# Broadcast load of the norm weights in the opening, two waits at seams placed otherwise, and 354 columns in two conv units: a hybrid conv and retention layer in fp32

## What is computed

```python
hn = rmsnorm(h, norm_mix_w)
proj = hn @ w_in                                   # 1024 x 3584
xt, b_gate, c_gate, q, k, v, g = jnp.split(proj, IN_SPLITS, axis=-1)
ucat = jnp.concatenate([conv_hist, c_gate * xt], axis=1)
conv_y = conv_w[0] * ucat[:, :T] + conv_w[1] * ucat[:, 1:T + 1] + conv_w[2] * ucat[:, 2:]
conv_out = b_gate * conv_y
...                                                # rotary q, k; chunked retention with decay; group norm
ret_out = jax.nn.silu(g) * o
h = h + jnp.concatenate([conv_out, ret_out], axis=-1) @ w_out
f = jnp.square(jax.nn.relu(rmsnorm(h, norm_ffn_w) @ w_up)) @ w_down
return h + f, new_hist, new_state
```

## Time and profile before

| | us |
|---|---|
| median of 3 runs (1237.04 to 1238.17) | 1237.44 |
| profiled execution, its own time | 1237.57 |
| its span from first to last instruction | 1235.3 |
| TensorE busy (99% of the span) | 1220.2 |
| TensorE weight loads | 1121.9 |
| DVE, ACT, POOL busy | 746.5, 494.7, 296.3 |
| TensorE's last matmul ends at about | 1226.6 |
| mean granted TensorE clock | 0.997 |

### The profile page before, as it was taken

The page is one execution under the profiler, slowest core; times in us unless marked ns, Lnnn a source line. Parts: engine busy times, 40 slices in busy tenths (PEclk is TensorE's granted clock), DMA queues, the critical chain, the costliest instruction groups (busy, mean ns, idle before and its releaser), DMA issues.

```text
span 1235.3 us, 20174 instructions
## 1 busy us (share of the span) xinstructions
PE 1220.2 (99%) x6674; PEld 1121.9 (91%) x6674; DVE 746.5 (60%) x1337; ACT 494.7 (40%) x1031; POOL 296.3 (24%) x230
## 2 busy tenths in 40 slices
PE   8999999999999999999999999999999999999997
PEld 5889999999999888989989989988998998998995
DVE  5435564465555453386676677568568667667747
ACT  5413213213232342355335435534543533543456
POOL 2000000000000000143543452352453354335212
PEclk9999999999999999999999999999999999999998
DMA  6011111111111630122021021111202202102103
GB/s 243 28 34 39 39 47 38 47 45 30 47 38 57 188 112 1 52 60 69 8 68 59 8 68 59 37 39 59 68 9 59 68 8 68 59 8 68 51 18 145
DMA packets 85117, 69.57 MB, mean 56 GB/s; under 512 B 9425, under 2 KB 68945, under 8 KB 85090
## 3 DMA queue, kind: packets, MB, share of 16 engines
q1 hardware_dynamic: 85090, 69.21, 18.2%
HBM read 64.21 MB, written 4.99 MB: 56 GB/s over the span
## 4 chain that ended last, share of the span: by engine, by line
PE 96%; DVE 2%; ACT 1%; issue 1%; DMA 1%; POOL 0%; POOLq 0%; SPq 0%; DVEq 0%; ACTq 0%
PE ps L1445 29%; PE ps L1447 29%; PE ps L1446 29%; PE ps L1451 1%; PE ps L1452 1%; PE ps L1462 1%; PE ps L1556 1%; PE ps L1633 1%; PE ps L1574 1%; PE ps L1563 1%; PE ps L1573 1%; PE ps L1469 0%; DMA dr<-in_w_down 0%; DVE hw L1353 0%; PE ps L1580 0%
## 5 line engine op out<-in xcount | busy, mean ns | idle before, releaser
L1445 PE MATMUL ps<-mid_hi,ws_hi 128*128 128x368 f32 (+1 forms) x768 | 251.3, 327 | 1.1 <-DVE ws_lo L1225 1.1
L1447 PE MATMUL ps<-mid_hi,ws_lo 128*128 128x368 f32 (+1 forms) x768 | 251.4, 327 | 0.0
L1446 PE MATMUL ps<-mid_lo,ws_hi 128*128 128x368 f32 (+1 forms) x768 | 250.8, 327 | 0.0
L1269 DVE TENSOR_TENSOR h<-ps,h 128x512 f32<-128x512 f32 x300 | 193.8, 678 | 8.5 <-PE ps L1447 8.5
L1445 PE MATMUL ps<-hn_hi,ws_hi 128*128 128x368 f32 (+1 forms) x576 | 194.4, 337 | 1.0 <-ACT v_all L616 1.0
L1447 PE MATMUL ps<-hn_hi,ws_lo 128*128 128x368 f32 (+1 forms) x576 | 189.5, 329 | 0.0
L1446 PE MATMUL ps<-hn_lo,ws_hi 128*128 128x368 f32 (+1 forms) x576 | 189.3, 329 | 0.0
L1393 POOL TENSOR_TENSOR h<-tmp,h 128x512 f32<-128x512 f32 x120 | 159.1, 1357 | 125.6 <-ACT tmp L817 125.6
L1445 PE MATMUL ps<-do_hi,fo_hi 128*128 128x512 f32 x452 | 176.2, 390 | 0.0
L1447 PE MATMUL ps<-do_hi,fo_lo 128*128 128x512 f32 x452 | 176.0, 389 | 0.0
L1446 PE MATMUL ps<-do_lo,fo_hi 128*128 128x512 f32 x452 | 176.0, 389 | 0.0
(11 more groups left out here) (198 smaller groups left out, 1826.1 us busy)
## 6 DMA issues: line engine op xcount, KB each, us to landing
raw<-in_w_up SPq DMA_DIRECT2D x64, 256.0 KB, 4.9
dr<-in_w_down SPq DMA_DIRECT2D x64, 256.0 KB, 3.5
raw<-in_w_in SPq DMA_DIRECT2D x48, 256.0 KB, 2.9
xr<-in_x_prompt SPq DMA_DIRECT2D x8, 512.0 KB, 4.0
raw<-in_w_out SPq DMA_DIRECT2D x16, 256.0 KB, 3.2
out<-hw SPq DMA_DIRECT2D x16, 256.0 KB, 2.1
wv_raw<-in_w_in SPq DMA_DIRECT2D x8, 256.0 KB, 5.2
h<-in_x_prompt SPq DMA_DIRECT2D x2, 1024.0 KB, 11.5
```

Source lines behind the costliest of these rows:

```text
L1269: dve.tensor_tensor(h_part(p, q), bank_of(p, q)[:, :], h_part(p, q), ALU.add).then_inc(dve_add, 1)
L1445: pe.matmul(out, a_hi, b_hi, start=start, stop=False, skip_group_check=again)
L1446: pe.matmul(out, a_hi, b_lo, start=False, stop=False, skip_group_check=again)
L1447: return pe.matmul(out, a_lo, b_hi, start=False, stop=stop, skip_group_check=again)
```

## The change

- The weights of the first norm are loaded by one broadcast DMA of 512 KB straight into `normw`, issued behind x tile 0. `norm_row`, `ones`, two matmuls and two DVE copies go; TensorE issues `keep_warm(5)` in place of 1 + 2 matmuls + 2.
- The order of the v weights' splits: ACT makes tile 0's hi parts after slice 1, then slices 2, 3, 4, then `root(1)`. DVE takes slices 0, 1, 2, 4, 6, POOL 3, 5, 7.
- TensorE waits for all but the last v tile ahead of the loop; the last one's wait stands before unit q, once in each turn of the loop.
- The memset of `h[:, 8]` moves ahead of the waits in `residual(4)`.
- ACT's group 0 is written out in front of its loop in an order of its own: relus of block 0 and the split of block 1's second half first, then all seven D splits.
- The last two meta rows are now the first two of the 16 in the row order (`META_AT`; positions and decays follow it, and x tile 8 comes in three DMAs). Units xt and c compute only these: their third column group is 354 wide in place of 368, and ACT and DVE copy 2 columns where they copied 16.

```diff
 CGQ = [(0, 368), (368, 368), (736, 352)]
+CGC = [(0, 368), (368, 368), (736, 354)]
+META_AT = [META - 2, META - 1, *range(META - 2)]
 CGY = [(0, 368), (368, 368), (736, 352)]
...
 UNITS = [("k", 3 * DC + DC, CGX), ("q", 3 * DC, CGQ), ("g", 3 * DC + 3 * DC, CGQ),
-         ("xt", 0, CGX), ("c", 2 * DC, CGX), ("b", DC, CGQ)]
+         ("xt", 0, CGC), ("c", 2 * DC, CGC), ("b", DC, CGQ)]
 V_OFF = 3 * DC + 2 * DC
+WV_DVE = [0, 1, 2, 4, 6]
+WV_POOL = [3, 5, 7]
 NU = len(UNITS)
...
     inv = (np.float32(10000.0) ** (-np.arange(half, dtype=np.float32) / np.float32(half))).astype(np.float32)
-    pos = np.concatenate([np.arange(SEQ), np.arange(SAMPLE) + PAST, np.arange(META) - META]).astype(np.float32)
+    pos = np.concatenate([np.arange(SEQ), np.arange(SAMPLE) + PAST, np.array(META_AT) - META]).astype(np.float32)
     ang = (pos[None, :] * inv[:, None]).astype(np.float32).astype(np.float64)
...
         head[h, :, C_KDEC] = np.exp((P - 1 - j) * lg) * scale
-        head[h, SAMPLE:SAMPLE + META, C_KMETA] = np.exp((META - 1 - j[:META]) * lg) * scale
+        head[h, SAMPLE:SAMPLE + META, C_KMETA] = np.exp((META - 1 - np.array(META_AT)) * lg) * scale
         head[h, :SAMPLE, C_KSAMP] = np.exp((SAMPLE - 1 - j[:SAMPLE]) * lg) * scale
...
             out = []
-            for src, a, b in ((xp_d, 0, SEQ), (xs_d, SEQ, TY), (meta_d, TY, TX)):
+            for src, a, b in ((xp_d, 0, SEQ), (xs_d, SEQ, TY), (meta_d[META - 2:META, :], TY, TY + 2), (meta_d[0:META - 2, :], TY + 2, TX)):
                 s, e = max(lo, a), min(hi, b)
...
-            sp.dma_start(norm_row[:, :], norm_mix_w[0:1, :]).then_inc(row_in, 16)
             load_x(0)
+            sp.dma_start(normw[:, :], norm_mix_w[0:1, :].broadcast_to([P, D])).then_inc(row_in, 16)
             sp.dma_start(ident[:, :], c_ident).then_inc(const_in, 16)
...
             wv_hi_part(1)
+            hi_parts(0)
             wv_hi_part(2)
-            hi_parts(0)
             wv_hi_part(3)
+            wv_hi_part(4)
             root(1)
-            for k in range(4, KT):
+            for k in range(5, KT):
                 wv_hi_part(k)
...
                     act.activation(u[:, META + SEQ + 2:TX + 2], bank[:, m:m + SAMPLE], ACT.Copy)
-                    act.activation(u[:, 0:META], bank[:, m + SAMPLE:n], ACT.Copy).then_inc(proj_act, 1)
+                    act.activation(u[:, META - 2:META], bank[:, m + SAMPLE:n], ACT.Copy).then_inc(proj_act, 1)
...
-            def group(g):
+            def group(g, first):
                 act.wait_ge(prod_done, NPROD * g + 1)
                 up_split(g, "up", 0)
-                d_hi(g, "B11")
-                d_hi(g, "T1")
-                d_hi(g, "B21")
-                d_hi(g, "T3")
-                act.wait_ge(f_ready, NF_PARTS * g + 1)
-                relu(g, 0, 0)
-                d_hi(g, "B22")
-                square(g, 0, 0)
-                relu(g, 0, 1)
-                d_hi(g, "T2")
-                relu(g, 0, 2)
-                up_split(g, "up", 1)
-                d_hi(g, "T4")
+                if first:
+                    relu(g, 0, 0)
+                    square(g, 0, 0)
+                    relu(g, 0, 1)
+                    relu(g, 0, 2)
+                    up_split(g, "up", 1)
+                    for name in D_HI:
+                        d_hi(g, name)
+                else:
+                    d_hi(g, "B11")
+                    d_hi(g, "T1")
+                    d_hi(g, "B21")
+                    d_hi(g, "T3")
+                    act.wait_ge(f_ready, NF_PARTS * g + 1)
+                    relu(g, 0, 0)
+                    d_hi(g, "B22")
+                    square(g, 0, 0)
+                    relu(g, 0, 1)
+                    d_hi(g, "T2")
+                    relu(g, 0, 2)
+                    up_split(g, "up", 1)
+                    d_hi(g, "T4")
                 square(g, 0, 1)
...
-            with act.Fori(0, G_LAST) as g:
-                group(g)
+            group(0, True)
+            with act.Fori(1, G_LAST) as g:
+                group(g, False)
...
             dve.memset(on[:, :, :], 0.0).then_inc(warm_ready, 1)
-            dve.memset(ones[:, :], 1.0).then_inc(warm_ready, 1)
...
-            dve.wait_ge(row_done, 1)
-            dve.tensor_copy(normw[:, 0:512], ps[1][:, :])
-            link(dve.tensor_copy(normw[:, 512:1024], ps[4][:, :]))
+            dve.wait_ge(row_in, 16)
             normed(0)
             wv_lo_part(0)
+            wv_lo_part(1)
             lo_parts(0)
             wv_lo_part(2)
+            wv_lo_part(4)
             normed(1)
-            wv_lo_part(4)
             wv_lo_part(6)
...
                         dve.tensor_tensor(u[:, META + SEQ + 2:TX + 2], bank[:, m:m + SAMPLE], u[:, META + SEQ + 2:TX + 2], ALU.mult)
-                        ins = dve.tensor_tensor(u[:, 0:META], bank[:, m + SAMPLE:n], u[:, 0:META], ALU.mult)
+                        ins = dve.tensor_tensor(u[:, META - 2:META], bank[:, m + SAMPLE:n], u[:, META - 2:META], ALU.mult)
                     ins.then_inc(proj_dve, 1)
...
                 n = rows(t)
+                if p == 4:
+                    dve.memset(h[SAMPLE:P, TILES - 1, :], 0.0)
                 dve.wait_ge(out_done, p + 1)
...
                     dve.wait_ge(h_rest_in, 32)
-                    dve.memset(h[SAMPLE:P, TILES - 1, :], 0.0)
                 pair = OUT_PAIRS[p]
...
             pool.memset(smC[:, :], 0.0).then_inc(pad_ready, 1)
-            for k in range(1, KT, 2):
+            for k in WV_POOL:
                 pool.wait_ge(wv_hi_ready, k + 1)
...
                     if t == 0:
-                        pe.wait_ge(wv_lo_pool if k % 2 else wv_lo_dve, k // 2 + 1)
+                        pe.wait_ge(wv_lo_pool, WV_POOL.index(k) + 1) if k in WV_POOL else pe.wait_ge(wv_lo_dve, WV_DVE.index(k) + 1)
                     elif k == 0 and t >= 2:
...
             pe.wait_ge(warm_ready, 1)
-            keep_warm(1)
-            pe.wait_ge(warm_ready, 2)
-            pe.wait_ge(row_in, 16)
-            pe.matmul(ps[1][:, :], ones[:, :], norm_row[:, 0:512], start=True, stop=True)
-            pe.matmul(ps[4][:, :], ones[:, :], norm_row[:, 512:1024], start=True, stop=True).then_inc(row_done, 1)
-            keep_warm(2)
+            keep_warm(5)
             pe.wait_ge(const_in, 16)
...
                 v_part(t, range(6, KT))
-            pe.wait_ge(v_taken, XTILES)
+            pe.wait_ge(v_taken, XTILES - 1)
...
                 elif name == "q":
+                    if j == 0:
+                        pe.wait_ge(v_taken, XTILES)
                     pe.wait_ge(proj_dve, i * 12 + 9 + j + 1)
```

More of the change, by code:

```diff
@@ L203, in build @@
         junk = sb("junk", [P, D], r3)
-        r_y = region(TY * 4)
-        y = sb("y", [P, TY], r_y)
-        norm_row = sb("norm_row", [1, D], r_y)
+        y = sb("y", [P, TY], region(TY * 4))
         cos_t = sb("cos_t", [P, TX], region(TX * 4))
@@ L216, in build @@
         onC = sb("onC", [P, HD], region(512))
-        r_rot = region(BLK * 4)
-        rot = sb("rot", [P, BLK], r_rot)
-        ones = sb("ones", [1, P], r_rot)
+        rot = sb("rot", [P, BLK], region(BLK * 4))
         hc = sb("hc", [P, NCONST], region(NCONST * 4))
@@ L250, in build @@
         row_in = sem("row_in")
-        row_done = sem("row_done")
         wv_in = [sem(f"wv_in{n}") for n in range(KT)]
```

## The result

| | before | after |
|---|---|---|
| median, us | 1237.57 (1237.04 to 1238.17, 6 runs) | 1228.97 (1228.24 to 1229.79, 6 runs) |
| ratio | | 0.9931, 95% interval 0.9918 to 0.9943 |
| profiled execution, its span | 1237.57, 1235.3 | 1229.5, 1227.3 |

The kernel is 8.6 us faster by the medians, 8.0 by the two spans. The forecast was 1232.1 with a range of 1228.8 to 1233.9: sign and range hold, the point is 3.1 us too high, and the time lies nearest to rival A, which gave 1230.0. The range holds by 0.2 us: its lower end had been set for rival A, not by the forecast's own terms.

A forecast was written before the change was run, and what follows sets the result against it. TensorE was taken as the bound from its start to its last matmul. Terms 0.6 + 1.0 + 1.1 + 0.2 + 1.3 + 1.2 = 5.4, off 1237.57 with another 0.1, gave 1232.1 us; 8-in-10 range 1228.8 to 1233.9.

The forecast's parts named there:

- rival A: Opening: TensorE's fast rate comes earlier once the one-row matmuls and holes go; 1230.0 us, chance 0.31.
- The opening: Start up to the first v matmul: norm weights by broadcast DMA let the transposes start 0.6 us earlier.
- The v matmuls of tile 0: First v matmul to tile 1's: new split order removes the wait for slice 4, shrinking 8.44 to 7.4, 1.0 us.
- The seam: Last v matmul to first unit: moving the wait for the last v tile's copy saves 1.1 us.
- the columns: Units xt and c: third column group 354 wide for 368 over 192 matmuls saves 1.2 us.
- group 0: First FFN group: ACT's earlier split removes TensorE's wait for ws_lo of up(1), half 1; 1.3 us.
- rival D: Conv units: 354-column fp32r matmuls might go at half rate, costing 28 us more; 1260 us, chance 0.03.
- rival C: Group 0: DVE's order together with POOL costs as much as T1 did, 1.3 less gain; 1233.4 us, chance 0.07.
- The memset: residual(4): the 0.91 us memset stays in DVE's chain to hw; at most 0.27 idle goes, gain 0.2 us.
- rival B: Opening gives nothing because broadcast or wv loads land late; seams and columns leave 3.8; 1233.5 us, chance 0.09.

The follow-up runs named there:

- one_row: Changed kernel with two one-row matmuls on zeros in the middle of the opening's keep_warm stream, in place of two full ones; measured 1231.80 us.
- rows64: As one_row, but the two matmuls in the middle of the opening stream use 64 rows; measured 1232.17 us.
- banks128: As one_row, but the two matmuls into the other banks use all 128 rows; measured 1228.84 us.
- warm3: Changed kernel with keep_warm(3) for keep_warm(5) ahead of the first transposes; measured 1228.17 us.
- open_row: Changed kernel with the norm row, its ones, two matmuls and DVE copies as before, the new split order and the rest kept; measured 1231.99 us.
- undo_cols: Changed kernel with the third column group of units xt and c at 368 columns again for 354; measured 1230.76 us.
- memset_early: Changed kernel with the memset of h[:, 8] moved between ht_lo(2) and ht_lo(3), out of residual(4); measured 1227.90 us.
- both: Changed kernel with the memset between ht_lo(2) and ht_lo(3) and keep_warm(4) for keep_warm(5); measured 1227.19 us.
- undo_group0: Changed kernel with ACT's first FFN group in the loop's order again; measured 1229.91 us.
- warm4: Changed kernel with keep_warm(4) for keep_warm(5) ahead of the first transposes; measured 1228.54 us.
- undo_seam: Changed kernel with TensorE waiting for all nine v tiles again ahead of the first unit; measured 1229.98 us.

## Why the prediction was right, and where not

The prediction was right in sign, range and in five of its six terms; the term that turned out largest was missed, and the sum stayed in range because rival A had been given room.

**The opening, 0.6 forecast, 2.94 measured.** This is the step that failed. Normed at 7.6 was forecast and came as 8.1; that TensorE and not the tile would be late was right. (The 9.56 of the earlier trace rows that the prediction calls normed is the start of the scaling; it ended at 10.84. With the transposes at 9.36 a tile that late would have held them, so the broadcast is needed for the gain too; this is argued, no run shows it alone.) The term put all ten records at 0.853 us and so their end at 10.83: it assumed that the lower rate would last as long as before. The argument against rival A, that full matmuls from 7.85 on had not raised the rate before 13 either, looked at how dense the stream was and not at what had run before. one_row, rows64 and banks128 show it: with the two partial matmuls between 4.1 and 7.9, the rise comes at 11 to 14 us (four traces, the kernel before among them), and in the streams of whole ones, in whatever bank, it had come by 8.3 (ten traces). Rival A named the two suspects, and its arithmetic (2.6 over the forecast for a rise at 7, 1.6 for one at 9) holds to 0.2 us: the rise came near 7.9, and 2.94 - 0.6 = 2.3. With hindsight its chance of 0.31 was low. The Trainium skill, page "TensorE: Matmul & The Clock Gate", Part 1, says that activity releases the throttle. The traces agree for every stream of whole matmuls here, where the rate rose 3.0 to 5.7 us after the start, or unseen in the pause of warm3.

**The v matmuls of tile 0, 1.0 forecast, 1.19 measured.** The stretch was laid out as 7.4 and took 7.25. The 1.84 us wait for slice 4 is gone, normed(1) is late next by 0.33, and slices 5 and 7 of POOL by 0.27 and 0.49 where 0.3 had been put. POOL's two subtracts took 3.86 together, 1.93 each, for the 1.7 taken. open_row shows that the gain is the order's own.

**The seam 1.1 (1.14), the columns 1.2 (1.22 with the out projection, 1.17 in undo_cols), group 0 1.3 (1.33)** came as worked out, and undoing each brought its stretch back. The 354 form runs at 323 ns between its neighbours of 352 and 368, so rival D has no ground. For group 0, `ws_lo` was forecast ready at least 0.8 ahead of need and was 0.9 ahead; rival C (DVE held up by POOL) is visible as 1.60 and 1.78 us for subtracts of 0.69, but short of the wait.

**The memset, 0.2 forecast, 0.0 measured.** The larger part was right: a memset moved inside its own step stays in the chain. The 0.27 us in front of it was taken for a wait that would go; it stayed, wherever the memset stood. memset_early, which takes it out of the chain, gains the 0.7.

The sum then reads 2.94 + 1.19 + 1.14 + 0.0 + 1.33 + 1.22 = 7.8 for 5.4, with 0.2 of small change elsewhere.

Two smaller slips of the working: rival B's 3.8 us give 1233.7 and not 1233.5, and the bounds of the terms, added up plainly, give 1231.0 to 1234.3 and not 1230.9 to 1233.3. Neither touches the result.

## What to carry to other kernels

Where TensorE gets work only to bring its rate up, whole matmuls of 128 rows without breaks are the safe choice: in this opening two matmuls of 1 or 64 rows among five cost 2.8 us or more by the medians against two whole ones in their place. A term for a stream in the opening needs both rates and a moment for the change, with what ran ahead of it in view, and a rival whose suspects both leave with the edit deserves as much weight as the forecast. Where TensorE is the bound and each wait has one cause, summing stretch by stretch got each term outside the opening within 0.2 us, and after each gain the next late engine has to be looked up: here a load and POOL's subtractions behind it took back 1.2 of 1.3 us in the profiled execution of one kernel.

## What the runs showed of the hardware

- The moment at which TensorE's rate rose varied from execution to execution of nearly the same opening: near 5.1 (both), 5.4 (undo_group0), 6.6 (warm4), 7.1 (undo_seam), 7.9 (after), worked out from the one distance between two records that lies between 0.85 and 0.43 us. With keep_warm(5) the first v matmul moved with it, from 11.46 (undo_group0) to 12.50 (after).
- The rate can also rise across a pause: in warm3 all six records ran at the lower rate and the transposes, behind 0.98 us of idle time, at the higher.
- The granted clock column of the profile shows nothing of this half rate: 1.00 in all slices from 0 to 14 us in one_row as in the changed kernel.
- A DVE subtract of two SBUF tiles took 0.69 us alone and 1.56 to 1.78 beside one of POOL, and POOL's went from 1.29 to as much as 1.93 (mean of two). The Trainium skill, page "SBUF — State Buffer", section "SBUF: two separate sides", says that a DVE instruction with two SBUF inputs and a GpSimd one that reads SBUF exclude each other on a shared pair of ports; the trace agrees: DVE's subtract at 515.33 met POOL's of 515.09 to 516.39, took 1.60 and ended 0.54 us behind it, while POOL's took its usual 1.30.
- A broadcast load of 512 KB to all partitions, issued behind another 512 KB, landed 5.4 us after its issue.
